# PEER decoder block on one core: tile 1's expert choice moved into the attention, a ring of 13 rows for the second gathered tile, later choices for the third

## What is computed

```python
q = einsum('bsd,dk->bsk', h, w_q).reshape(b, s, 8, 2, 128)
scores = einsum('bshcd,hcnd->bshcn', q, sub_keys)          # 128 keys per half
s1, i1 = top_k(scores[..., 0, :], 16); s2, i2 = top_k(scores[..., 1, :], 16)
cand = s1[..., :, None] + s2[..., None, :]                 # 256 pairs per head
top_s, pos = top_k(cand, 16); ids = take(i1*128 + i2, pos) # 128 experts per token
gates = softmax(top_s)
act = gelu(einsum('td,tkd->tk', h, u_tab[ids])) * gates    # 16384 experts of 1024 values
ffn = einsum('tk,tkd->td', act, v_tab[ids])
```

## Time and profile before

| | |
|---|---|
| median of 3 runs | 3259.27 us |
| the profiled execution's own time | 3262.99 us |
| its span | 3261.2 us |
| VectorE, TensorE, POOL busy | 68%, 82%, 45% of the span |
| first DMA of the third block | 913.16 us |
| step 0, 2, 6 of the third block: first query multiply | 917.5, 942.0, 1025.1 us |
| dense chunk 0 and 16: ScalarE's GELU | 1355.0, 1643.5 us |
| last V gather | 3213.5 us |

### The profile page before, as it was taken

The page is one execution under the profiler, slowest core; times in us unless marked ns, Lnnn a source line. Parts: engine busy times, 40 slices in busy tenths (PEclk is TensorE's granted clock), DMA queues, the critical chain, the costliest instruction groups (busy, mean ns, idle before and its releaser), DMA issues.

```text
span 3261.2 us, 30907 instructions
## 1 busy us (share of the span) xinstructions
PE 2669.5 (82%) x9137; PEld 1364.6 (42%) x9137; DVE 2201.8 (68%) x4895; ACT 559.1 (17%) x1267; POOL 1482.6 (45%) x1333
## 2 busy tenths in 40 slices
PE   8999994675668887657689999999999987878883
PEld 3454542443324555423334444444444443434441
DVE  3334577867648788678845766744444688888888
ACT  1231101332103777400000000100000000000000
POOL 0011004445334222344565555566656576675773
PEclk9999996887888899878889999999999989889996
DMA  4213226555479898898999999899999999999995
GB/s 146 87 52 139 91 84 231 178 199 194 187 285 344 310 331 320 296 358 313 331 394 373 385 376 404 326 407 398 396 404 397 377 407 407 406 407 371 404 409 191
DMA packets 310549, 987.81 MB, mean 303 GB/s; under 512 B 29936, under 2 KB 57840, under 8 KB 309616
## 3 DMA queue, kind: packets, MB, share of 16 engines
q0 software_dynamic: 184320, 671.17, 54.1%
q1 hardware_dynamic: 123440, 314.21, 25.6%
q10 hardware_dynamic: 2624, 0.46, 0.1%
HBM read 947.98 MB, written 37.75 MB: 302 GB/s over the span
## 4 chain that ended last, share of the span: by engine, by line
PE 24%; issue 15%; POOL 14%; DMA 10%; DVE 5%; ACT 2%; DVEq 1%; ACTq 1%; PEld 0%; POOLq 0%; PEldq 0%
POOL u_ring L1994 9%; PE part L2090 7%; PE hid L2071 6%; PE turn_ps L2063 4%; DMA v_ring<-in_peer_v_dram,ids_t 4%; PE acc L2128 4%; POOL v_ring L2021 4%; DMA v_ring<-in_peer_v_dram,ids_u 2%; DVE x_rows_in L2317 2%; POOL v_ring L2007 2%; PE part L2099 1%; ACT dense_sums L2168 1%; DMA u_ring<-in_peer_u_dram,ids_u 1%; DMA u_ring<-in_peer_v_dram,ids_t 1%; ACT dense_sums L2170 1%
## 5 line engine op out<-in xcount | busy, mean ns | idle before, releaser
L2090 PE MATMUL part<-room 128*128 128x512 f32 x1536 | 716.4, 618 | 198.1 <-DVE room L2398 186.2
L2422 DVE CUSTOM_DVE_ANT_0 u_ring<-u_ring,x_rows_in 128x1024 f32<-128x1024 f32 x512 | 618.7, 1223 | 314.9 <-DMA u_ring<-in_peer_u_dram,ids_u 305.2
L1994 POOL DMA_INDIRECT u_ring<-in_peer_u_dram,ids_u x512 | 580.0, 1133 | 469.3 <-DVE dots L2422 327.1
L2071 PE MATMUL hid<-x1t_dense,room 128*128 128x384 f32 x2048 | 692.6, 492 | 5.8 <-DMA room<-in_peer_ut_dram 4.6
L2007 POOL DMA_INDIRECT v_ring<-in_peer_v_dram,ids_t x344 | 368.1, 1070 | 384.3 <-PE acc L2128 269.9
L2090 PEld LDWEIGHTS part<-room 128*128 128x128 f32 x1536 | 302.2, 199 | 565.6 <-issue 346.0
L2071 PEld LDWEIGHTS hid<-x1t_dense,room 128*128 128x128 f32 x2048 | 387.4, 192 | 320.9 <-issue 80.8
L2317 DVE SCALAR_TENSOR_TENSOR x_rows_in<-v_ring,coef,x_rows_in 128x1024 f32<-128x1024 f32 x208 | 267.1, 1284 | 63.8 <-DMA v_ring<-in_peer_v_dram,ids_u 50.1
L2206 ACT ACTIVATE room<-hid 128x384 f32<-128x384 f32 x128 | 62.7, 490 | 1435.0 <-PE hid L2071 1435.0
L2021 POOL DMA_INDIRECT v_ring<-in_peer_v_dram,ids_u x208 | 234.7, 1129 | 76.5 <-issue 58.5
L1165 POOL DMA_INDIRECT u_rows<-in_peer_u_dram,ids_first x123 | 153.0, 1244 | 186.7 <-POOLq L1164 160.9
(11 more groups left out here) (368 smaller groups left out, 2809.0 us busy)
## 6 DMA issues: line engine op xcount, KB each, us to landing
room<-in_peer_ut_dram SPq DMA_DIRECT2D x128, 512.0 KB, 7.0
room<-in_peer_v_dram SPq DMA_DIRECT2D x128, 512.0 KB, 9.7
wq_pair<-in_peer_wq_dram SPq DMA_DIRECT2D x25, 2048.0 KB, 19.0
gate_grid<-room SPq DMA_DIRECT2D x6, 4096.0 KB, 13.8
room<-gate_grid SPq DMA_DIRECT2D x32, 768.0 KB, 17.3
w_ring<-in_w_in_dram SPq DMA_DIRECT2D x10, 2048.0 KB, 7.9
w_ring<-in_w_out_dram SPq DMA_DIRECT2D x4, 2048.0 KB, 8.2
u_ring<-in_peer_u_dram,ids_u POOLq DMA_INDIRECT x512, 10.6
```

The lines of the kernel that those rows point to most:

```text
L1994: pool.indirect_dma_start(u_ring[:, n % U_RING, :], None, peer_u, bass.IndirectOffsetOnAxis(ap=ids_u[:, q, k:k + 1], axis=0))\
L2071: last = mm.matmul(hid[:, 0:DT], ud[:, c % UD_RING, k, :], x1td[:, k, :], start=(k == 0), stop=(k == KC - 1))
L2090: last = mm.matmul(part[k % 3][:], weights[:, n % 2, i, d * P:(d + 1) * P], vd[:, slot, half * 512:(half + 1) * 512], start=(i == 0), stop ...
L2422: vec.tensor_tensor_reduce(u_ring[:, n % U_RING, :], u_ring[:, n % U_RING, :], x1[:, q % 2, :], 1.0, 0.0, ALU.mult, ALU.add, dots[:, q % 2 ...
```

## The change

Three things. First, tile 1's choice leaves the third block. It is made in the attention: `choice(n, lag)` starts pair g at step 15 + 4g, with stages one step apart: query multiply, turning, keys on TensorE, copies on ScalarE, then on VectorE `best_eight` and `next_eight` at lag 4 and `best_pairs` and `look_up` at lag 5. SP loads the four pairs' weights there. To make room, the products are 3 a step in steps 0 to 27 and 4 a step after that, so they end in step 38 and not 31. The third block then starts with tile 2's choice: `STEPS` is 149, choices without marks are steps 0 and 1, both together 2 to 11, marks alone 12 and 13, `DENSE_AT` = 14, `EARLY_TURNS` = 4. Tile 0's V quads come in steps 2 to 12, two and then three a step. Second, tile 4's U rows go through 13 buffers, `u_ring` and `v_ring` together (`u_place`); the first V rows of tile 4 in `v_ring` wait until all 128 are used. Third, tile 5's pairs are chosen at steps 24, 28, 32, 36, and POOL waits for each pair (`pairs_chosen`) in place of the whole tile; its U rows begin at step 30.

```diff
-        SPARE_FROM = 4 * (items + 2)
+        SPARE_FROM = 3 * items + 4 * 2
...
+        def choice(n, lag):
+            g, rest = divmod(n - CHOICE - lag, DA_HEADS)
+            return g if rest == 0 and 0 <= g < HEADS // 2 else None
...
+        def products_by(n):
+            return 3 * min(n, items) + 4 * max(n - items, 0)
...
+                    if choice(n, 4) is not None:
+                        dve.wait_ge(pair_for_dve, 1).then_inc(pair_for_dve, -1)
+                        best_eight(vec, dve, pairs, sc_one).then_inc(pair_free, 1)
+                        next_eight(vec, dve, pairs)
+                    if (g := choice(n, 5)) is not None:
+                        at = slice(g * 2 * TOPK, (g + 1) * 2 * TOPK)
+                        best_pairs(vec, dve, pairs, top_one[:, at].rearrange("p (h k) -> p h k", k=TOPK))
+                        look_up(vec, dve, pairs, picks_one[:, :, at].rearrange("p c (h k) -> p h c k", k=TOPK))
                     for k in products(n):
...
-CHOSEN_AT = {1: 0, 2: 4, 3: 8, 4: 12, 5: 20, 6: 40, 7: 43}
+CHOSEN_AT = {2: 0, 3: 4, 4: 8, 5: 24, 6: 39, 7: 42}
-EARLY_TURNS = 7
-DENSE_AT = 18
+EARLY_TURNS = 4
+DENSE_AT = 14
-V_COUNTS = (2 * (3,) + 13 * (2,), (2,) + 30 * (1,), (2,) + 30 * (1,))
+V_COUNTS = ((2,) + 10 * (3,), (2,) + 30 * (1,), (2,) + 30 * (1,))
...
+DEEP_ROWS = SLOTS
+DEEP_RING = U_RING + V_RING
+def u_place(n):
+    return n % DEEP_RING if n < DEEP_ROWS else n % U_RING
...
             def gather_u(n, q, k):
-                if n >= U_RING:
-                    pool.wait_ge(u_used, n - U_RING + 1)
+                if row_before(n) is not None:
+                    pool.wait_ge(u_used, row_before(n) + 1)
...
             def gather_v(m, q, s, j):
+                if m in (WIDE_QUADS, WIDE_QUADS + 1):
+                    pool.wait_ge(u_used, DEEP_ROWS)
```

More of the change, by code:

```diff
@@ L123, in build_mixer @@
                 d_skip, ssd_norm_g, ln1_g, ln1_b, x1_dram, x1t_dram, peer_wq, keys_t, peer_u,
-                ids_first, top_first, dots_first, wq_pair, keys_pair, kept):
+                ids_first, top_first, dots_first, wq_pair, keys_pair, rows_kept, kept):
     vec, act_, mm = nc.vector, nc.scalar, nc.tensor
@@ L1042, in build_mixer @@
         rstd = sb("rstd1", [P, 1])
+        x1t_one = q_t[:, :, 6 * P:8 * P].rearrange("p h (i n) -> p h i n", i=2)
+        q_one = q_t[:, :, 0:P]
+        sc_one = rows_kept[:, 3 * SLOTS:3 * SLOTS + 2 * DKEY]
+        pairs = PairChoice(sb, "_one", k_t[:, :, 6 * P:8 * P])
+        iota_one = sb("iota_one", [P, TOPK], I32)
+        x1t_one_ready = handshake("x1t_one_ready")
+        q_done = handshake("q_done_one")
+        q_copied = handshake("q_copied_one")
+        qt_done = handshake("qt_done_one")
+        qt_copied = handshake("qt_copied_one")
+        pair_scored = handshake("pair_scored_one")
+        pair_for_pe = handshake("pair_for_pe_one")
         u_rows = sb("u_rows", [P, U_FIRST_RING, D])
@@ L1221, in _ @@
                         scores(n)
+                    if choice(n, 0) is not None:
+                        if choice(n, 0) == 0:
+                            pe.wait_ge(x1t_one_ready, 1).then_inc(x1t_one_ready, -1)
+                        pe.wait_ge(wq_in, 16).then_inc(wq_in, -16)
+                        pe.wait_ge(op_free, 1).then_inc(op_free, -1)
+                        for c in range(KC):
+                            last = mm.matmul(OP[:], x1t_one[:, c // 2, c % 2, :], wq_pair[:, c, :], start=(c == 0), stop=(c == KC - 1))
+                        last.then_inc(q_done, 1)
+                    if choice(n, 1) is not None:
+                        pe.wait_ge(q_copied, 1).then_inc(q_copied, -1)
+                        for c in range(4):
+                            last = mm.transpose(OP[:, c * P:(c + 1) * P], q_one[:, c, :], ident[:])
+                        last.then_inc(qt_done, 1)
+                    if choice(n, 2) is not None:
+                        pe.wait_ge(qt_copied, 1).then_inc(qt_copied, -1)
+                        pe.wait_ge(keys_in, 16).then_inc(keys_in, -16)
+                        for c in range(4):
+                            at = slice(c * P, (c + 1) * P)
+                            last = mm.matmul(OP[:, at], q_one[:, c, :], keys_pair[:, at], start=True, stop=True)
+                        last.then_inc(pair_scored, 1)
                     if tail(n, 13) is not None:
@@ L1245, in _ @@
                         for half in range(2):
-                            if half and t >= 3:
+                            if half == 0 and choice(n, 3) is not None:
+                                pe.wait_ge(pair_for_pe, 1).then_inc(pair_for_pe, -1)
+                            elif half and t >= 3:
                                 pe.wait_ge(t_free[1], 1).then_inc(t_free[1], -1)
@@ L1303, in _ @@
                         act.sem_inc(mix_ready, 1)
+                    if choice(n, 0) is not None:
+                        act.wait_ge(q_done, 1).then_inc(q_done, -1)
+                        act_.activation(q_one, OP[:].rearrange("p (c n) -> p c n", c=4), ACT.Copy).then_inc(q_copied, 1)
+                    if choice(n, 1) is not None:
+                        act.wait_ge(qt_done, 1).then_inc(qt_done, -1)
+                        act_.activation(q_one, OP[:].rearrange("p (c n) -> p c n", c=4), ACT.Copy).then_inc(qt_copied, 1)
+                    if choice(n, 2) is not None:
+                        act.wait_ge(pair_scored, 1).then_inc(pair_scored, -1)
+                        act.sem_inc(wq_free, 1)
+                        act.wait_ge(pair_free, 1).then_inc(pair_free, -1)
+                        act_.activation(sc_one, OP[:], ACT.Copy)
+                        act.drain().then_inc(pair_for_pe, 1)
+                        act.sem_inc(pair_for_dve, 1)
             @block.vector
@@ L1308, in _ @@
                 dve.sem_inc(rows_free, U_FIRST_RING)
+                dve.wait_ge(iota_ready, 1).then_inc(iota_ready, -1)
+                vec.tensor_copy(pairs.iota16[:], iota_one[:])
                 for n in range(last_step + 1):
@@ L1564, in v_slots, with u_rows_in, row_before @@
     return group, wide_uses(group) + use + 1, m - 1 if use else last + 1
-def u_rows_landed(m, j):
-    rows = U_BASE[1] if m < WIDE_QUADS else U_BASE[-1] + SLOTS
-    return (rows - j + U_RING - 1) // U_RING
-def u_uses(n):
-    slot = n % U_RING
-    return n // U_RING + 1 + (wide_uses(2) if n >= U_BASE[1] and slot < 4 else 0)
+DEEP_ROWS = SLOTS
+DEEP_RING = U_RING + V_RING
+def u_place(n):
+    return n % DEEP_RING if n < DEEP_ROWS else n % U_RING
+def u_rows_in(place, rows):
+    return sum(u_place(n) == place for n in range(rows))
+def u_uses(n):
+    place = u_place(n)
+    quads = wide_uses(2) * (place < 4) if place < U_RING else wide_uses((place - U_RING) // 4)
+    return u_rows_in(place, n + 1) + quads
+def row_before(n):
+    return max((m for m in range(n) if u_place(m) == u_place(n)), default=None)
 def share(items, i, n):
@@ L1592, in chosen_pair, with turn_of @@
     return None
+def turn_of(t, pair):
+    return next(n for n, turn in enumerate(TURNS) if turn[1:] == (t, pair))
 def weight_loads(n):
@@ L1612, in chosen_step @@
 def chosen_step(t):
-    if t == 0:
-        return -1
+    if t in CHOSEN_IN_MIXER:
+        return t - 1
     if t == FOLLOWER:
@@ L1836, in build_experts, with u_row, u_row_landed @@
         consts = sem("consts2_e")
+        def u_row(n):
+            place = u_place(n)
+            return u_ring[:, place, :] if place < U_RING else v_ring[:, place - U_RING, :]
+        def u_row_landed(n):
+            place = u_place(n)
+            return u_landed[place] if place < U_RING else v_landed[place - U_RING]
         def last_row(i):
@@ L2443, in _ @@
                         choose(*turn)
-                        if turn[0] == 3 and turn[3] == PAIRS - 1:
-                            dve.sem_inc(tiles_chosen, 1)
+                        if turn[0] == 3:
+                            dve.sem_inc(pairs_chosen, 1)
                 if u_ended(s, 0) is not None:
```

93 lines of the change are left out of this document (56 added, 37 removed).

## The result

The change takes 3222.56 us, the median of 4 runs (3218.93 to 3227.67), beside 3259.0 us for the kernel before: a ratio of 0.9885, 95% interval 0.9869 to 0.9900. The forecast was 3205, with a range of 3160 to 3254. So it is faster, by 36 us and not by 54.

| us | before | after | difference | forecast |
|---|---|---|---|---|
| start to the third block's first DMA | 913.2 | 963.8 | +50.7 | +38 |
| from there to chunk 0 | 441.8 | 372.1 | -69.7 | -67 |
| chunk 0 to chunk 16 | 288.5 | 236.9 | -51.6 | -40 |
| chunk 16 to the end | 1617.7 | 1649.4 | +31.7 | +15 |

What follows compares the result with a forecast made beforehand. No engine was full in the attention; from 913 us the DMA engines were busy 0.95 of the time, with TensorE busy late. From 3259.27 us, 38 - 67 - 40 + 15 = -54 gave 3205 us, range 3160 to 3254.

Steps and rivals of the forecast that it cites:

- The attention, +38: Attention with tile 1's choice added: 38 us longer, from -15 early, +19 for two pairs, +34 in the tail.
- the 2.62 us wait: VectorE's wait for scores in the attention's projection step: predicted to go, with 3 us taken off, leaving 9.5 us a pair.
- The early steps: Attention before step 19: 13 steps that VectorE paces, 1.15 us gained in each, 15 us in all.
- the tail: End of the attention: 107 us of VectorE work, 114 us long, 34 more than before, with VectorE the last engine.
- Steps 0 to 13, -67: Start of the third block: 83 us of choices without marks go, 16 us of prices come back, 67 us shorter.
- The first sixteen chunks, -40: First sixteen dense chunks: 40 us shorter, down toward a transfer floor of 234 us from 288, less new wait and unevenness.
- the new wait: Tile 4's first V rows wait until all 128 U rows are used: 8 us more, counted in the first sixteen chunks.
- Both of its causes: First sixteen chunks: 13 buffers remove most of 64.2 us of VectorE's waits; two choices moved out remove another 29.6.
- The rest, +15: From the seventeenth chunk on: order kept, two of tile 5's pairs added beside chunks 18 and 22, 15 us longer.
- The transfers as the pace: Rival: third block keeps its mean of 365 GB/s, so the kernel gets 12 us slower, 3271 us; chance 0.14.
- More is gained: Rival: mark steps stay at 27.5 us, chunks reach their floor, attention costs +25; 97 us faster, 3162 us; chance 0.14.
- the ring brings nothing: Rival: gathers held up on POOL at 1.99 us each, so first chunks gain 0; 14 us faster, 3245 us; chance 0.14.

Runs made afterwards that it cites:

- `choice(n, 7)`: The changed kernel with best_pairs and look_up of a pair at lag 7 in place of lag 5, in the projection's step; 3209.94 us, ratio 0.9839.
- the square: Four kernels, tile 4's U rows through 5 or 13 buffers, choices at places of before or later: 5 buffers 3248.16 and 3246.11 us, 13 buffers 3214.55 and 3222.56.
- the ring of 5: The changed kernel with tile 4's U rows through five buffers again and its V rows no longer waiting for all 128; 3246.11 us, ratio 0.9958.
- three of the faster kernels: Not identified by name; late losses are reported for pairs five steps apart (3213.90 us), 117 rows in the 13 buffers (3215.78) and three edits together (3215.61).
- The same twelve products: The changed kernel with four more products in each of attention steps 10, 14, 18: ahead of reading the projection's first half 3231.73 us, behind it 3211.70.

## Why the prediction was right or wrong

**The attention, +38: right in sign, 13 us too small.** The step that failed is "While VectorE is in these steps, TensorE gets ahead, and the 2.62 us wait goes: I take 3 us off, 9.5 us a pair". It doesn't get ahead. In step 21 of the change TensorE and VectorE read:

```profile
762.94 1.30 PE L1237 MATMUL bank<-ident,probs 128*128 128x128 f32 x5 [12.49 <-PEq L1235]
...
767.56 1.13 PE L1226 MATMUL wide<-k_t,q_t 64*128 64x512 f32 x4
```

```profile
761.63 0.75 DVE L1403 SCALAR_TENSOR_TENSOR probs<-probs,ratio 128x512 f32<-128x512 f32 x1
...
769.25 0.69 DVE L1388 TENSOR_REDUCE neg_mx<-wide 128x1 f32<-128x512 f32 x1 [3.19 <-DVEq L1386]
```

TensorE turns the weights that VectorE combined in the same step (the combination ends at 762.4), and the next scores stand behind that turning in its queue. So the late VectorE makes TensorE late by as much, and the wait is 3.19 us (2.76 in the second group), not gone. Without those 3 us the term is 12.5 a pair, and 12.8 and 13.4 were measured: 7 of the 13 us. The early steps gave 12 us and not 15 (2 of them already ahead of the first step), and the tail cost 36 for 34. In the tail the working held: VectorE busy 104.6 us where 107 were counted, and it is the last engine. That each pair "adds 14.8 us to the two steps that VectorE paces" was read rightly; that its second half need not stand there was tested by `choice(n, 7)`.

**Steps 0 to 13, -67: right.** From the first multiply to chunk 0 it took 367.6 us where 370 were named. The mark steps moved 370 GB/s, the bound that was named, at a share of 0.96, and the query weights landed in 13.7 us (median of nine), between the two bounds of the earlier trace rows:

```profile
wq_pair<-in_peer_wq_dram SPq DMA_DIRECT2D x9, 2048.0 KB, 13.7
```

**The first sixteen chunks, -40: right in mechanism, nearly at its better end.** The floor that the transfers set was put at 234 us, and 236.9 were measured at 391 GB/s. The 8 us for the new wait were counted here and fell behind chunk 16, as 7 us, and only beside a moved pair: with them the term is -44.5. Both of its causes count here, 33.5 and 23 us alone and 50 together, as the square shows. What wasn't set against the second is its price behind chunk 16, the whole of the next term: in the total the moved choices bring nothing with the ring of 5 and cost 8 us with the ring of 13.

**The rest, +15: measured +32.** Without the 7 us of the step from chunk 16 to 17 it is +25. Of these the two added pairs are 16, 8 each, where 15 were counted for both. The step that failed is "Everything from the seventeenth chunk on keeps its order, but two of tile 5's pairs now fall into it, beside chunks 18 and 22". Beside chunk 22 a pair stood before as well; the second added one is tile 7's last, beside chunk 46. What wasn't counted is whom VectorE's half of the last one delays: it stands right before tile 5's coefficients, and chunks 48 and 49 take the other 8 us longer. I had asked TensorE's price of a moved pair and not VectorE's at its new place.

**The total.** In the profiled executions it lies 15 us off, as errors of +13 and +17 stand beside -3 and -12. Some 7 us of the +17 and of the -12 are one and the same wait, counted one row too early; what is left is +13 and +10 against -3 and -5, so luck has a small part in it.

**The rivals.** The transfers as the pace decide at a mean under 367 GB/s; it was 375. Whether the 4 to 6 us that are lost late in three of the faster kernels are theirs stays open. *More is gained* was right for the chunks, which reached 236.9 us of its 234, and wrong for the attention, +51 and not +25. That the ring brings nothing is refuted by the ring of 5. Its mechanism, gathers held up on POOL, is there in part. Line 2105 in the first chunks of the change (duration ns min/median/max):

```profile
L2105 POOL DMA_INDIRECT v_ring<-in_peer_u_dram,ids_u x78: 934/1250/1991, 1312.3 to 1548.9; - x78
L2105 POOL DMA_INDIRECT u_ring<-in_peer_u_dram,ids_u x50: 932/942/1988, 1305.6 to 1537.4; - x50
...
DMA to landing us min/median/max: 4.2/16.1/25.4
```

The median into `v_ring` is 1250 ns where the earlier trace rows had 938; it would have had to be 1991 throughout. The Trainium skill, SBUF — State Buffer, section SBUF: two separate sides, says that VectorE and GpSimd share a pair of ports that certain of their instructions hold to themselves. It gives no reason for the difference between the buffers, and whether the longer gathers come from those ports no run here shows. The figure of the Trainium skill, Perfetto Trace Analysis, section Roofline, some 435 GB/s for 16 DMA engines, wasn't held over any stretch here: a share of 1.00 was 391, and 404 at a share of 1.03 is the most in the rows above. Only single windows of 7 us in the mark steps show more (467 GB/s from 1044.2 to 1051.5 us of the change).

## What to carry to other kernels

Work that moves to another engine's idle time is priced at its place in the queue: ask for each half which engine paces that step, and what stands behind it on its own queue that another engine waits for. The same twelve products cost 9 us or gave 11, and the same half of a choice cost 8.9 or 2.6 us, by a few lines of order. Where an edit feeds a starved stage by moving work out of it, price the work at its new place for every engine: the moved choices saved 16 to 23 us in the first chunks and cost 25 to 32 behind them.
